# Where the split weights of eleven projections stand in SBUF, seen from the split activations

## The chip, the cores and the metric

One core of one Trainium2 chip runs the whole program. The metric is device time in microseconds (us) of that core; less is better.

## The reference

Two transformer-like blocks on one sequence of 512 tokens with 1024 features, all in float32. The first block has a sparse-attention mixer with gates, a feed-forward network, a gated linear recurrence and a second feed-forward network; the second has differential attention, a mixture of experts, an RWKV mixer and a second mixture of experts. Between them stand large dense projections of the form `h @ w`, and eleven of them are what this case is about:

```
proj = h @ w_in                     # nsa_in:  1024 -> 2560 (+48 gates)
o @ w_out                           # nsa_out: 1024 -> 1024
silu(h @ w_gate) * (h @ w_up)       # ffn_in, twice:  1024 -> 2 x 2816
(...) @ ffn_w_out                   # ffn_out, twice: 2816 -> 1024
h @ w_in                            # rg_in:   1024 -> 2 x 1408
(...) @ w_out                       # rg_out:  1408 -> 1024
x @ w_qkv                           # da_in:   1024 -> 3072
o @ w_o                             # da_out:  1024 -> 1024
(y * g) @ w_o                       # rw_out:  1024 -> 1024
```

## The kernel before

Everything is kept transposed: features on the 128 partitions, in chunks of 128, and the 512 tokens along the free dimension. A projection is computed by the helper `dense` (line 128). To get float32 accuracy out of float32r matmuls it splits both operands into a high part (a float32r copy) and a low part (what is left): weights into `whi` and `wlo`, activations into `xhi` and `xlo`. Per chunk of 128 input features and 128 output features it issues three matmuls of 128x128 weights against 128x512 activations into one PSUM bank: high by high (line 212), high weights by low activations (line 213), low weights by high activations (line 214):

```
nc.tensor.matmul(ps[0:width, slot * tiles + o], high, xhi[:, k], start=(k == 0), stop=False)
nc.tensor.matmul(ps[0:width, slot * tiles + o], high, xlo[:, k], start=False, stop=False)
last = nc.tensor.matmul(ps[0:width, slot * tiles + o], low, xhi[:, k], start=False, stop=(k == kt - 1))
```

Each matmul is preceded by the load of its own weights, which TensorE does while the matmul before it streams its activations. The weights are the stationary operand (128 columns of 4 bytes, 512 bytes of a partition), the activations the moving one (512 columns, 2048 bytes).

The weights come tile by tile, n tiles a projection, in two slots. SyncE issues the DMA of a tile once the slot's last split is done; ScalarE copies it into `whi[:, slot]`; VectorE subtracts that into `wlo[:, slot]`; TensorE waits for the split (`lo_done`), multiplies, and signals `products_done`; ScalarE or VectorE takes the result from PSUM. A projection can have a head: the first chunks of its first tile, split earlier into tiles of their own (`early.hi` and `early.lo`, named nsa_in_h0, da_in_h0 and so on), so that it can begin without a wait. `stay_busy` (line 329) issues bf16 matmuls of 512 columns before a projection.

Tiles are placed in SBUF in the order in which the code asks for them, each behind the one before (a few from the right end). Where a tile stands, in bytes of a partition modulo 512, is called its line here. The distance is that of `whi` or `wlo` from `xhi` and `xlo`, modulo 512. All four are whole multiples of 512 bytes long, chunk by chunk as well, so one distance holds for all chunks of a projection. Before the change it is 0 in all eleven. In the feed-forward network an unused tile sees to that: between `xlo` and `whi` stand 32 bytes of a coefficient tile, 4096 of `silu` and 480 of `ffn{layer}_to_line` (line 613), together 4608, nine times 512. A similar one, `rg_to_line` (line 1240), stands in the recurrence. The heads stand at 0 as well, but for that of da_in, which lies at the right end: da_in_h0 at byte 219104 and da_in_xhi at 174624, which is 448 modulo 512.

Three other groups of float32r matmuls with 512 columns play a part in the prediction, all in the compression stage after nsa_in. The gate projection (lines 774 to 776) has 48 columns a chunk, so its weights step by 192 bytes while the activations step by 2048; the first chunk stands at 0. The headed spreads (lines 757 and 758) multiply a 24x128 one-hot tile, `cp_heads`, with the split reciprocals `cp_rhi` and `cp_rlo`; the distance is 128 throughout.

Of the kernel before, what the change touches and what calls it, by code (L numbers as in the profile page):

```python
# [14 lines left out]
F32 = mybir.dt.float32  # L15
# [4 lines left out]
P = 128  # L20
SEQ = 512
D = 1024
KD = D // P
# [6 lines left out]
KR = RNN // P  # L30
# [94 lines left out]
                sp.dma_start(dst, src).then_inc(self.second_loaded, 16)  # L125


def dense(B, name, n, tiles, kt, kp, width, loads, x, act_body=None, dve_body=None, unrolled=False, xhi=None, xlo=None, is_split=False, pool_body=None, dve_head=None, norm=None, early=None, sp_tail=None, slots=None, coming=None, busy=(0, 0, 0)):

# [10 lines left out]
    nc, ACT, ALU = B.nc, B.ACT, B.ALU  # L142
    with ExitStack() as st:
        if slots is None:
            w2 = st.enter_context(nc.sbuf_tensor(name + "_w", [kp, 2, kt, tiles * width], F32))
            slots = (w2[:, 0], w2[:, 1])
        whi = st.enter_context(nc.sbuf_tensor(name + "_whi", [kp, 2, kt, tiles * width], F32R))
        wlo = st.enter_context(nc.sbuf_tensor(name + "_wlo", [kp, 2, kt, tiles * width], F32R))
        if xhi is None:
            xhi = st.enter_context(nc.sbuf_tensor(name + "_xhi", [kp, kt, SEQ], F32R))  # L150
        if xlo is None:
            xlo = st.enter_context(nc.sbuf_tensor(name + "_xlo", [kp, kt, SEQ], F32R))
# [425 lines left out]
def add_mixed(B, layer, part, tiles=2):  # L578

    nc, ALU = B.nc, B.ALU  # L580

    def body(dve, i, slot, ps):
        for o in range(tiles):
            x = B.xT[:, bass.ds(i * tiles + o, 1)]
            nc.vector.scalar_tensor_tensor(out=x, in0=ps[:, o:o + 1], scalar=B.gate_col(layer, part, i * tiles + o), in1=x,
                                           op0=ALU.mult, op1=ALU.add)
    return body


def ffn(B, layer, next_weights=None):  # L590
    nc, A, ACT, ALU = B.nc, B.A, B.ACT, B.ALU
    w_in = A["ffn_w_in"][layer].rearrange("(k p) n -> p k n", p=P)
    w_out = A["ffn_w_out"][layer].rearrange("(k p) n -> p k n", p=P)
    KF = FFN // P
    with ExitStack() as st:

        with ExitStack() as s2:
            normed = s2.enter_context(nc.sbuf_tensor(f"ffn{layer}_normed", [P, KD, SEQ], F32))
            rstd = s2.enter_context(nc.sbuf_tensor(f"ffn{layer}_rstd", [P, SEQ], F32))
        hhi = st.enter_context(nc.sbuf_tensor(f"ffn{layer}_hhi", [P, KF, SEQ], F32R))  # L600
        hlo = st.enter_context(nc.sbuf_tensor(f"ffn{layer}_hlo", [P, KF, SEQ], F32R))

        came = st.enter_context(nc.sbuf_tensor(f"ffn{layer}_came", [P, 2 * KD * 2 * P], F32))
        in_slots = tuple(came[:, q * KD * 2 * P:(q + 1) * KD * 2 * P].rearrange("p (k n) -> p k n", k=KD) for q in range(2))
        out_first = came[:, 0:KF * P].rearrange("p (k n) -> p k n", k=KF)
        out_loads = lambda w, i: [(w[:, :, :], w_out[:, :, bass.ds(i * P, P)])]
        early = EarlyWeights(B, f"ffn{layer}_out", st, KF, P, out_loads, out_first, head=KD)
        with ExitStack() as s2:
            xhi = s2.enter_context(nc.sbuf_tensor(f"ffn{layer}_xhi", [P, KD, SEQ], F32R))
            xlo = s2.enter_context(nc.sbuf_tensor(f"ffn{layer}_xlo", [P, KD, SEQ], F32R))  # L610
            norm = RmsModulate(B, f"n2_{layer}", s2, "norm2_g", layer, 3, normed, rstd[:])
            gated = s2.enter_context(nc.sbuf_tensor(f"ffn{layer}_silu", [P, 2, SEQ], F32))
            s2.enter_context(nc.sbuf_tensor(f"ffn{layer}_to_line", [P, 120], F32))
            h = gated
            h_chain = B.sem(f"ffn{layer}_h_chain")

            def loads(w, i):
                return [(w[:, :, 0:P], w_in[:, :, bass.ds(i * P, P)]),
                        (w[:, :, P:2 * P], w_in[:, :, bass.ds(i * P + FFN, P)])]

            def product(dve, i, slot, ps):
                nc.vector.tensor_tensor(h[:, slot], gated[:, slot], ps[:, 1], ALU.mult).then_inc(h_chain, 1)  # L622
                dve.wait_ge(h_chain, i * 2 + 1)
                row = lambda T: T[:, bass.ds(i, 1)].rearrange("p o t -> p (o t)")
                nc.vector.tensor_copy(row(hhi), h[:, slot]).then_inc(h_chain, 1)
                dve.wait_ge(h_chain, i * 2 + 2)
                nc.vector.tensor_tensor(row(hlo), h[:, slot], row(hhi).bitcast(F32), ALU.subtract)
            dense(B, f"ffn{layer}_in", KF, 2, KD, P, P, loads, None, busy=(6, 3, 8),
                  act_body=lambda i, slot, ps: nc.scalar.activation(gated[:, slot], ps[:, 0], ACT.Silu),  # L629
                  dve_body=product, xhi=xhi, xlo=xlo, norm=norm, sp_tail=early.load, slots=in_slots, coming=early)  # L630
        out_second = st.enter_context(nc.sbuf_tensor(f"ffn{layer}_out_w1", [P, KF, P], F32))
        coming = next_weights() if next_weights else None
        dense(B, f"ffn{layer}_out", KD, 1, KF, P, P,
              out_loads, None, dve_body=add_mixed(B, layer, 5, tiles=1), xhi=hhi, xlo=hlo, is_split=True, early=early, slots=(out_first, out_second[:]),
              sp_tail=coming.load if coming else None, coming=coming)


def nsa(B):
# [6 lines left out]
    nc, A, ACT, ALU = B.nc, B.A, B.ACT, B.ALU  # L645
    w_in = A["nsa_w_in"][0].rearrange("(k p) n -> p k n", p=P)
# [10 lines left out]
    with ExitStack() as st:  # L657
# [7 lines left out]
        norm = RmsModulate(B, "n1_0", x_scope, "norm1_g", 0, 0, projT[:, 12:20], projT[:, 11], summed_early=True)  # L665
# [16 lines left out]
        def clear(pool):  # L682
# [3 lines left out]
            for T in (kcz, vcz):  # L686
                nc.gpsimd.memset(T[:], 0.0)

        dense(B, "nsa_in", 10, 2, KD, P, P, loads, None, busy=(0, 0, 8), unrolled=True, xhi=xhi, xlo=xlo, norm=norm, early=early, pool_body=clear, sp_tail=small_loads,
              act_body=lambda i, slot, ps: nc.scalar.activation(projT[:, 2 * i:2 * i + 2], ps, ACT.Copy))  # L690


# [235 lines left out]
        out_first = st.enter_context(nc.sbuf_tensor("nsa_out_w2", [P, KD, 256], F32))  # L928
        early = EarlyWeights(B, "nsa_out", st, KD, 256, out_loads, head=KD // 2, second=True)
        nsa_attention(B, projT, kz, kcz, vnat, vcz, gates, ohi, olo, early)  # L930
        dense(B, "nsa_out", 4, 2, KD, P, P, out_loads, None, dve_body=add_mixed(B, 0, 2), xhi=ohi, xlo=olo, is_split=True, early=early, slots=(out_first[:], early.second[:]))


def nsa_attention(B, projT, kz, kcz, vnat, vcz, gates, ohi, olo, early):
# [279 lines left out]
def rg_lru(B):  # L1214
# [7 lines left out]
    with ExitStack() as st:  # L1222
# [11 lines left out]
        xhi = yhi[:, 0:KD]  # L1234
# [75 lines left out]

        def pad(dve):
            nc.vector.memset(raw[:, :, 0:PAD], 0.0).then_inc(conv_chain, 1)
        dense(B, "rg_in", KR, 2, KD, P, P, busy=(3, 3, 12), loads=lambda w, i: [(w[:, :, 0:P], w_in[:, :, i * P:(i + 1) * P]),
                            (w[:, :, P:2 * P], w_in[:, :, i * P + RNN:(i + 1) * P + RNN])],
              x=None, act_body=take, dve_body=convolve, xhi=xhi, xlo=xlo, unrolled=True, norm=RmsModulate(B, "n1_1", x_scope, "norm1_g", 1, 0, gT[:, 0:KD], conv[:, KR - 1]), pool_body=load_band, dve_head=pad, slots=(came[:].rearrange("p (k n) -> p k n", k=KD), in_second[:]))
        x_scope.close()
# [1 line left out]
        with ExitStack() as s2:  # L1318
# [144 lines left out]
            def _(dve):  # L1463
# [56 lines left out]
                                            B.cols("ada_b", (8 + h) * KD, KD).rearrange("p (t j) -> p t j", j=2), ALU.add)  # L1520
        scope.close()
        dense(B, "rg_out", KD, 1, KR, P, P,
              out_loads, None, busy=(0, 0, 3), dve_body=add_mixed(B, 1, 2, tiles=1), xhi=yhi, xlo=ylo, is_split=True, early=early)


ALPHA = (2 * 2) ** 0.25
# [2 lines left out]
def add_deepnorm(B):  # L1529

    nc, ALU = B.nc, B.ALU

    def body(dve, i, slot, ps):
        x = B.xT[:, bass.ds(i * 2, 2)]
        return nc.vector.scalar_tensor_tensor(out=x, in0=x, scalar=ALPHA, in1=ps, op0=ALU.mult, op1=ALU.add)
    return body


def qkv_loads(B):
    w_qkv = B.A["attn_w_qkv_2"][0].rearrange("(k p) n -> p k n", p=P)  # L1540
    return lambda w, i: [(w[:, :, :], w_qkv[:, :, bass.ds(i * 256, 256)])]
# [36 lines left out]
def diff_attention(B, early_in, right):  # L1578
# [8 lines left out]
    with ExitStack() as st:  # L1587
# [4 lines left out]
        with ExitStack() as s2:  # L1592
            sb = lambda name, shape: s2.enter_context(nc.sbuf_tensor("da_" + name, shape, F32))
            projT = sb("projT", [P, 24, SEQ])
            odd = right.enter_context(nc.sbuf_tensor("da_in_w1", [P, KD, 256], F32, side="right"))
            dense(B, "da_in", 12, 2, KD, P, P, qkv_loads(B), B.xT, early=early_in, slots=(early_in.w[:], odd[:]),
                  act_body=lambda i, slot, ps: nc.scalar.activation(projT[:, bass.ds(i * 2, 2)], ps, ACT.Copy, scale=SC if i < 4 else 1.0),
                  unrolled=True)
            right.close()
# [173 lines left out]
            def _(dve):  # L1773
# [84 lines left out]
        units = right.enter_context(nc.sbuf_tensor("da_moe_units", [P, AHEAD, HID // P, D], F32, side="right"))  # L1858
        B.ahead = [units[:, u] for u in range(AHEAD)]
        dense(B, "da_out", KD // 2, 2, KD, P, P,  # L1860
              out_loads, None, busy=(0, 0, 3), dve_body=add_deepnorm(B), xhi=ohi, xlo=olo, is_split=True, early=early, sp_tail=lambda sp: ask_gate_and_up(B, sp, 0, B.ahead))


def norm_moe(B, layer, gain, bias, mixer=None):
# [1099 lines left out]
def rwkv(B, dest, gate, AR):  # L2964
# [11 lines left out]
    with ExitStack() as st:  # L2976
# [22 lines left out]
        def out_loads(wt, i):  # L2999
# [3 lines left out]
        early = EarlyWeights(B, "rw_out", st, KD, 256, out_loads, tile=quarters(Bt)[:, 0], head=KD // 2)  # L3003
        B.ahead = [AR[:, u].rearrange("p (k a) n -> p k (a n)", a=2) for u in range(AHEAD)]
        rwkv_result(B, AR, K, Vn, bonus, mixed_g, g_w1, ohi, olo, early)
        dense(B, "rw_out", KD // 2, 2, KD, P, P, out_loads, None, busy=(0, 0, 3), dve_body=add_deepnorm(B), xhi=ohi, xlo=olo, is_split=True, early=early,
              slots=(quarters(K)[:, 0], quarters(K)[:, 1]), sp_tail=lambda sp: ask_gate_and_up(B, sp, 1, B.ahead))


# [616 lines left out]
```

## Time and profile before

| what | value |
|---|---|
| median of 3 runs | 3282.23 us (3279.44 to 3285.97) |
| span of the profiled execution | 3277.8 us |
| time of the profiled execution around its span | not given; the median is 4.4 us over the span |
| TensorE busy | 2920.2 us, 89% |
| VectorE, ScalarE, GpSimd busy | 1310.6, 887.2, 264.2 us |
| mean granted TensorE clock | 0.956 |

The span is that of one execution, from the first to the last instruction. Matmul durations overlap, since a matmul enters the array while the one before it is still draining; the time from one start to the next is the rate at which they are done. Starts in the order of time are given to 0.01 us, so rates are read over several matmuls. The granted clock is a share of 2.4 GHz.

### The profile page before, as it was taken

The numbers are of one execution on the slowest core, as the hardware profiler recorded it, in microseconds if no ns is written. First come the engines' busy times: TensorE is split into PE (matmuls) and PEld (weight loads), VectorE is DVE, ScalarE is ACT, GpSimd is POOL, SyncE is SP. The second block draws the span as 40 slices with busy tenths as digits, with TensorE's granted clock in tenths as the row PEclk, the third lists the DMA queues.
The fourth block names the chain that finished last, engine by engine and source line by source line (L and its number), as shares of the span: only waits on it lengthen the run. The fifth ranks groups of instructions, "written<-read, shape, count | busy, mean of one in ns | idle before, by whom it ended". The sixth has DMA issues, their size and how long they took to land. (4 is left out here: it accounts for less than half of the span.)

```text
span 3277.8 us, 66493 instructions
## 1 busy us (share of the span) xinstructions
PE 2920.2 (89%) x27826; PEld 2116.8 (65%) x27826; DVE 1310.6 (40%) x2356; ACT 887.2 (27%) x1564; POOL 264.2 (8%) x344
## 2 busy tenths in 40 slices
PE   7999999999998999999988997775888998997876
PEld 5766678878764788787756664443467866664453
DVE  3265543331656433322374221112596564221213
ACT  3245522221445222212362000003342333000002
POOL 1014300000400000000000000001121430000001
PEclk9999999999998999999999999887899999999998
DMA  8335233331426333423307999998122217999997
GB/s 211 79 113 200 75 80 95 97 101 53 121 64 228 85 100 94 109 66 103 110 25 285 375 396 427 425 428 312 39 58 81 47 33 288 391 426 425 426 426 293
DMA packets 378062, 638.64 MB, mean 195 GB/s; under 512 B 90693, under 2 KB 327922, under 8 KB 343802
## 3 DMA queue, kind: packets, MB, share of 16 engines
q1 hardware_dynamic: 352329, 601.98, 50.4%
q10 hardware_dynamic: 21264, 23.88, 2.1%
q0 software_dynamic: 4256, 9.68, 0.8%
q8 instruction: 166, 2.72, 0.3%
q14 instruction: 47, 0.38, 0.0%
HBM read 611.06 MB, written 24.38 MB: 194 GB/s over the span
## 5 line engine op out<-in xcount | busy, mean ns | idle before, releaser
L2296 DVE TENSOR_TENSOR moe_scratch<-moe_scratch,moe_ps 128x128 f32<-128x128 f32 x102 | 39.4, 386 | 652.6 <-ACT moe_scratch L2153 652.6
L212 PE MATMUL ffn_in_ps<-ffn_xhi,ffn_in_whi 128*128 128x512 f32 x704 | 274.4, 390 | 6.3 <-DVE ffn_xlo L417 4.5
L2095 PE MATMUL moe_ps<-moe_ring,moe_scratch 128*32 128x256 f32 x3360 | 213.4, 404 | 69.0 <-DMA moe_ring<-in_moe_w_gu 58.3
L213 PE MATMUL ffn_in_ps<-ffn_xlo,ffn_in_whi 128*128 128x512 f32 x704 | 274.1, 389 | 0.0
L214 PE MATMUL ffn_in_ps<-ffn_xhi,ffn_in_wlo 128*128 128x512 f32 x704 | 274.0, 389 | 0.0
L2095 PEld LDWEIGHTS moe_ps<-moe_ring,moe_scratch 128*32 128x32 f32 x3360 | 126.0, 115 | 150.6 <-issue 63.0
L2080 PE MATMUL moe_ps<-xT,moe_hot 128*32 128x256 f32 x3296 | 202.6, 384 | 0.0
L2153 ACT ACTIVATE moe_scratch<-moe_ps 128x128 f32<-128x128 f32 x102 | 28.3, 277 | 503.7 <-PE moe_ps L2095 501.7
L2080 PEld LDWEIGHTS moe_ps<-xT,moe_hot 128*32 128x32 f32 x3296 | 122.4, 113 | 62.2 <-issue 8.7
L212 PEld LDWEIGHTS ffn_in_ps<-ffn_xhi,ffn_in_whi 128*128 128x128 f32 x704 | 132.2, 188 | 35.3 <-issue 5.4
L213 PEld LDWEIGHTS ffn_in_ps<-ffn_xlo,ffn_in_whi 128*128 128x128 f32 x704 | 132.2, 188 | 27.4
L214 PEld LDWEIGHTS ffn_in_ps<-ffn_xhi,ffn_in_wlo 128*128 128x128 f32 x704 | 132.2, 188 | 27.3
L622 DVE TENSOR_TENSOR ffn_silu<-ffn_silu,ffn_in_ps 128x512 f32<-128x512 f32 x44 | 30.3, 688 | 282.1 <-ACT ffn_silu L629 282.1
L2095 PE MATMUL moe_ps<-da_moe_units,moe_scratch 128*32 128x256 f32 x1600 | 107.6, 421 | 37.0 <-DMA da_moe_units<-in_moe_w_gu 33.7
L2157 ACT ACTIVATE moe_y<-moe_ps 128x256 f32<-128x256 f32 x102 | 39.1, 383 | 356.1 <-PE moe_ps L2105 356.1
L2105 PE MATMUL moe_ps<-moe_ring,moe_scratch 128*32 128x256 f32 x1952 | 119.4, 383 | 16.4 <-issue 16.0
L213 PE MATMUL ffn_out_ps<-ffn_hlo,ffn_out_whi 128*128 128x512 f32 x336 | 130.8, 389 | 0.0
L212 PE MATMUL ffn_out_ps<-ffn_hhi,ffn_out_whi 128*128 128x512 f32 x336 | 130.8, 389 | 0.0
L214 PE MATMUL ffn_out_ps<-ffn_hhi,ffn_out_wlo 128*128 128x512 f32 x336 | 130.8, 389 | 0.0
L629 ACT ACTIVATE ffn_silu<-ffn_in_ps 128x512 f32<-128x512 f32 x44 | 26.3, 597 | 359.2 <-PE ffn_in_ps L214 359.2
L2095 PE MATMUL moe_ps<-rw_AR,moe_scratch 128*32 128x256 f32 x1504 | 94.5, 400 | 28.5 <-DMA rw_AR<-in_moe_w_gu 25.2
L2095 PEld LDWEIGHTS moe_ps<-da_moe_units,moe_scratch 128*32 128x32 f32 x1600 | 62.7, 119 | 76.5 <-issue 35.0
(788 smaller groups left out, 6006.1 us busy)
## 6 DMA issues: line engine op xcount, KB each, us to landing
moe_ring<-in_moe_w_gu SPq DMA_DIRECT2D x74, 2048.0 KB, 36.6
moe_ring<-in_moe_w_down SPq DMA_DIRECT2D x38, 2048.0 KB, 34.8
da_moe_units<-in_moe_w_gu SPq DMA_DIRECT2D x27, 2048.0 KB, 31.2
rw_AR<-in_moe_w_gu SPq DMA_DIRECT2D x27, 2048.0 KB, 29.0
ffn_came<-in_ffn_w_in SPq DMA_DIRECT2D x88, 512.0 KB, 5.0
da_moe_units<-in_moe_w_down SPq DMA_DIRECT2D x13, 2048.0 KB, 37.4
rw_AR<-in_moe_w_down SPq DMA_DIRECT2D x13, 2048.0 KB, 33.4
na_modw<-in_ada_w SPq DMA_DIRECT2D x6, 4096.0 KB, 13.6
```

The lines of the kernel that those rows point to most:

```text
L212: nc.tensor.matmul(ps[0:width, slot * tiles + o], high, xhi[:, k], start=(k == 0), stop=False)
L213: nc.tensor.matmul(ps[0:width, slot * tiles + o], high, xlo[:, k], start=False, stop=False)
L214: last = nc.tensor.matmul(ps[0:width, slot * tiles + o], low, xhi[:, k], start=False, stop=(k == kt - 1))
L622: nc.vector.tensor_tensor(h[:, slot], gated[:, slot], ps[:, 1], ALU.mult).then_inc(h_chain, 1)
L629: act_body=lambda i, slot, ps: nc.scalar.activation(gated[:, slot], ps[:, 0], ACT.Silu),
L2080: last = nc.tensor.matmul(psX[j * BLK:(j + 1) * BLK].rearrange("p (q n) -> p q n", q=2), hot[:, c], rows_of(c)[:, j::4], start=(c == 0), s ...
L2095: last = nc.tensor.matmul(psGU[j * BLK:(j + 1) * BLK].rearrange("p (g a n) -> p g a n", g=2, a=2), xbT[:, k], cols[:, j], start=(k == 0), ...
L2105: last = nc.tensor.matmul(psY[j * BLK:(j + 1) * BLK], hT[:, k * BLK:(k + 1) * BLK], unit(PARTS * e + 2)[:, k, j * 256:(j + 1) * 256], star ...
L2153: nc.scalar.activation(gated, psG, ACT.Silu).then_inc(silu_done, 1)
L2157: nc.scalar.activation(y[:, s], psY, ACT.Copy).then_inc(y_taken, 1)
L2296: V.tensor_tensor(h.rearrange("p (a m i) -> p a i m", a=2, m=2), gated.rearrange("p (a i m) -> p a i m", a=2, m=2), psU.rearrange("p (a i ...
```

## The change

`dense` gets a parameter `apart`, two numbers of bytes. The first is left unused ahead of `whi`, the second ahead of `wlo`; where `dense` places `xhi` itself, as in da_in alone of the eleven, it leaves as much again ahead of `xhi` as brings that back to its line. The tile `ffn{layer}_to_line` goes. The calls pass these values:

```diff
+        def leave(what, line):
+            if line:
+                st.enter_context(nc.sbuf_tensor(f"{name}_before_{what}", [kp, line // 4], F32))
+        leave("whi", apart[0])
         whi = st.enter_context(nc.sbuf_tensor(name + "_whi", [kp, 2, kt, tiles * width], F32R))
+        leave("wlo", apart[1])
         wlo = st.enter_context(nc.sbuf_tensor(name + "_wlo", [kp, 2, kt, tiles * width], F32R))
         if xhi is None:
+            leave("xhi", (1024 - apart[0] - apart[1]) % 512 if apart[0] + apart[1] else 0)
             xhi = st.enter_context(nc.sbuf_tensor(name + "_xhi", [kp, kt, SEQ], F32R))
...
-            s2.enter_context(nc.sbuf_tensor(f"ffn{layer}_to_line", [P, 120], F32))
...
 ffn_in:   apart=(32, 0) if layer == 0 else (416, 0)
 ffn_out:  apart=(256, 0) if layer == 0 else (96, 0)
 nsa_in:   apart=(128, 0)
 nsa_out:  apart=(384, 0)
 rg_in:    apart=(192, 0)
 rg_out:   apart=(320, 0)
 da_in:    apart=(0, 256)
 da_out:   apart=(256, 256)
 rw_out:   apart=(160, 0)
```

(The last nine lines list the new argument of each call; nothing else in the calls changes.) The heads' own tiles keep their places, and so do the raw weight tiles, the activations handed to `dense`, and everything outside it. The RWKV input projections have code of their own and are not touched.

## Rows read from the trace of the kernel before

**Rows 1.** The page, parts 1 and 2: TensorE's busy time, by 40 slices

```profile
PE 2920.2 (89%) x27826; PEld 2116.8 (65%) x27826; DVE 1310.6 (40%) x2356; ACT 887.2 (27%) x1564; POOL 264.2 (8%) x344
...
PE   7999999999998999999988997775888998997876
```

**Rows 2.** Windows over the projections, three rows and the header; the sum is of eleven

```profile
core 0: us, PE busy (x) PEld busy (x) DVE busy (x) ACT busy (x) POOL busy (x), PEclk, DMA share, GB/s
...
455.40:690.00 234.60, 233.68 (x1030) 193.30 (x1031) 93.91 (x98) 57.16 (x50) 0.00 (x0) 1.00 0.34 95
...
1495.30:1619.20 123.90, 123.90 (x548) 102.38 (x546) 22.94 (x10) 29.35 (x21) 0.00 (x0) 1.00 0.23 75
...
sum 1253.50, PE 1248.75 PEld 1030.84 DVE 429.03 ACT 286.31 POOL 23.08; mean PE 113.52 PEld 93.71 DVE 39.00 ACT 26.03 POOL 2.10
```

**Rows 3.** Line 214: who waited for it (us, times)

```profile
  ACT ffn_silu L629: 359.2, 44
```

**Rows 4.** Line 212 on TensorE: counts, durations in ns (min/median/max), first and last start

```profile
L212 PE MATMUL ffn_in_ps<-ffn_xhi,ffn_in_whi x704: 387/389/497, 455.4 to 1356.8; 128*128 128x512 f32 x176
L212 PE MATMUL ffn_out_ps<-ffn_hhi,ffn_out_whi x336: 388/389/390, 706.2 to 1481.2; 128*128 128x512 f32 x168
L212 PE MATMUL da_in_ps<-da_in_xhi,da_in_whi x188: 388/389/767, 1488.2 to 1618.5; 128*128 128x512 f32 x188
L212 PE MATMUL rg_in_ps<-rg_yhi,rg_in_whi x176: 388/389/766, 833.4 to 953.8; 128*128 128x512 f32 x176
L212 PE MATMUL nsa_in_ps<-nsa_xhi,nsa_in_whi x146: 388/389/398, 56.1 to 154.7; 128*128 128x512 f32 x146
L212 PE MATMUL rg_out_ps<-rg_yhi,rg_out_whi x88: 388/389/497, 1042.8 to 1102.1; 128*128 128x512 f32 x88
L212 PE MATMUL nsa_out_ps<-nsa_ohi,nsa_out_whi x56: 388/389/394, 399.5 to 439.6; 128*128 128x512 f32 x56
L212 PE MATMUL da_out_ps<-da_ohi,da_out_whi x56: 388/389/395, 1718.8 to 1758.9; 128*128 128x512 f32 x56
L212 PE MATMUL rw_out_ps<-rw_ohi,rw_out_whi x56: 388/389/390, 2711.9 to 2752.0; 128*128 128x512 f32 x56
```

**Rows 5.** In order of time, da_in's first tile; 1493.77 to 1495.14 loads the head

```profile
1493.77 0.39 PE L214 MATMUL da_in_ps<-da_in_xhi,da_in_wlo 128*128 128x512 f32 x1
...
1495.14 0.39 PE L214 MATMUL da_in_ps<-da_in_xhi,da_in_l 128*128 128x512 f32 x1
...
1501.94 0.39 PE L214 MATMUL da_in_ps<-da_in_xhi,da_in_wlo 128*128 128x512 f32 x1
```

**Rows 6.** Groups of instructions, 1493.9 to 1495.3 us (busy us, mean ns)

```profile
L213 PE MATMUL da_in_ps<-da_in_xlo,da_in_h 128*128 128x512 f32 x2 | 0.8, 394 | 0.0
L212 PE MATMUL da_in_ps<-da_in_xhi,da_in_h 128*128 128x512 f32 x2 | 0.8, 392 | 0.0
```

**Rows 7.** In order of time, the gate projection, second and last of its 24 matmuls

```profile
162.83 0.39 PE L775 MATMUL cp_psT<-nsa_xlo,cp_whi_g 128*48 128x512 f32 x1
...
167.88 0.39 PE L776 MATMUL cp_psT<-nsa_xhi,cp_wlo_g 128*48 128x512 f32 x1
```

**Rows 8.** In order of time, rg_out after a stall: matmuls 2, 8 and 15

```profile
1043.13 0.39 PE L213 MATMUL rg_out_ps<-rg_ylo,rg_out_whi 128*128 128x512 f32 x1
...
1044.52 0.39 PE L213 MATMUL rg_out_ps<-rg_ylo,rg_out_whi 128*128 128x512 f32 x1
...
1046.11 0.39 PE L214 MATMUL rg_out_ps<-rg_yhi,rg_out_wlo 128*128 128x512 f32 x1
```

**Rows 9.** In order of time, headed spreads, second and last of a run of 8

```profile
189.72 0.38 PE L758 MATMUL cp_psD<-cp_rlo,cp_heads 24*128 24x512 f32 x1
...
191.12 0.39 PE L758 MATMUL cp_psD<-cp_rlo,cp_heads 24*128 24x512 f32 x1
```

**Rows 10.** In order of time, six of the helper's bf16 matmuls

```profile
451.32 1.46 PE L332 MATMUL ffn_in_ps<-ident_b 128*128 128x512 bf16 x6
```

**Rows 11.** Groups of instructions, 451.1 to 452.75 us (busy us, mean ns)

```profile
L332 PE MATMUL ffn_in_ps<-ident_b 128*128 128x512 bf16 x7 | 1.7, 379 | 0.0
```

More of the change, by code:

```diff
@@ L125, in load, with dense @@
                 sp.dma_start(dst, src).then_inc(self.second_loaded, 16)
-def dense(B, name, n, tiles, kt, kp, width, loads, x, act_body=None, dve_body=None, unrolled=False, xhi=None, xlo=None, is_split=False, pool_body=None, dve_head=None, norm=None, early=None, sp_tail=None, slots=None, coming=None, busy=(0, 0, 0)):
+def dense(B, name, n, tiles, kt, kp, width, loads, x, act_body=None, dve_body=None, unrolled=False, xhi=None, xlo=None, is_split=False, pool_body=None, dve_head=None, norm=None, early=None, sp_tail=None, slots=None, coming=None, busy=(0, 0, 0), apart=(0, 0)):
     nc, ACT, ALU = B.nc, B.ACT, B.ALU
@@ L627, in product @@
                 nc.vector.tensor_tensor(row(hlo), h[:, slot], row(hhi).bitcast(F32), ALU.subtract)
-            dense(B, f"ffn{layer}_in", KF, 2, KD, P, P, loads, None, busy=(6, 3, 8),
+            dense(B, f"ffn{layer}_in", KF, 2, KD, P, P, loads, None, busy=(6, 3, 8), apart=(32, 0) if layer == 0 else (416, 0),
                   act_body=lambda i, slot, ps: nc.scalar.activation(gated[:, slot], ps[:, 0], ACT.Silu),
@@ L633, in ffn @@
         dense(B, f"ffn{layer}_out", KD, 1, KF, P, P,
-              out_loads, None, dve_body=add_mixed(B, layer, 5, tiles=1), xhi=hhi, xlo=hlo, is_split=True, early=early, slots=(out_first, out_second[:]),
+              out_loads, None, apart=(256, 0) if layer == 0 else (96, 0), dve_body=add_mixed(B, layer, 5, tiles=1), xhi=hhi, xlo=hlo, is_split=True, early=early, slots=(out_first, out_second[:]),
               sp_tail=coming.load if coming else None, coming=coming)
@@ L687, in clear @@
                 nc.gpsimd.memset(T[:], 0.0)
-        dense(B, "nsa_in", 10, 2, KD, P, P, loads, None, busy=(0, 0, 8), unrolled=True, xhi=xhi, xlo=xlo, norm=norm, early=early, pool_body=clear, sp_tail=small_loads,
+        dense(B, "nsa_in", 10, 2, KD, P, P, loads, None, apart=(128, 0), busy=(0, 0, 8), unrolled=True, xhi=xhi, xlo=xlo, norm=norm, early=early, pool_body=clear, sp_tail=small_loads,
               act_body=lambda i, slot, ps: nc.scalar.activation(projT[:, 2 * i:2 * i + 2], ps, ACT.Copy))
@@ L930, in nsa @@
         nsa_attention(B, projT, kz, kcz, vnat, vcz, gates, ohi, olo, early)
-        dense(B, "nsa_out", 4, 2, KD, P, P, out_loads, None, dve_body=add_mixed(B, 0, 2), xhi=ohi, xlo=olo, is_split=True, early=early, slots=(out_first[:], early.second[:]))
+        dense(B, "nsa_out", 4, 2, KD, P, P, out_loads, None, apart=(384, 0), dve_body=add_mixed(B, 0, 2), xhi=ohi, xlo=olo, is_split=True, early=early, slots=(out_first[:], early.second[:]))
 def nsa_attention(B, projT, kz, kcz, vnat, vcz, gates, ohi, olo, early):
@@ L1312, in pad @@
             nc.vector.memset(raw[:, :, 0:PAD], 0.0).then_inc(conv_chain, 1)
-        dense(B, "rg_in", KR, 2, KD, P, P, busy=(3, 3, 12), loads=lambda w, i: [(w[:, :, 0:P], w_in[:, :, i * P:(i + 1) * P]),
+        dense(B, "rg_in", KR, 2, KD, P, P, apart=(192, 0), busy=(3, 3, 12), loads=lambda w, i: [(w[:, :, 0:P], w_in[:, :, i * P:(i + 1) * P]),
                             (w[:, :, P:2 * P], w_in[:, :, i * P + RNN:(i + 1) * P + RNN])],
@@ L1522, in rg_lru @@
         dense(B, "rg_out", KD, 1, KR, P, P,
-              out_loads, None, busy=(0, 0, 3), dve_body=add_mixed(B, 1, 2, tiles=1), xhi=yhi, xlo=ylo, is_split=True, early=early)
+              out_loads, None, apart=(320, 0), busy=(0, 0, 3), dve_body=add_mixed(B, 1, 2, tiles=1), xhi=yhi, xlo=ylo, is_split=True, early=early)
 ALPHA = (2 * 2) ** 0.25
@@ L1595, in diff_attention @@
             odd = right.enter_context(nc.sbuf_tensor("da_in_w1", [P, KD, 256], F32, side="right"))
-            dense(B, "da_in", 12, 2, KD, P, P, qkv_loads(B), B.xT, early=early_in, slots=(early_in.w[:], odd[:]),
+            dense(B, "da_in", 12, 2, KD, P, P, qkv_loads(B), B.xT, apart=(0, 256), early=early_in, slots=(early_in.w[:], odd[:]),
                   act_body=lambda i, slot, ps: nc.scalar.activation(projT[:, bass.ds(i * 2, 2)], ps, ACT.Copy, scale=SC if i < 4 else 1.0),
@@ L1860, in diff_attention @@
         dense(B, "da_out", KD // 2, 2, KD, P, P,
-              out_loads, None, busy=(0, 0, 3), dve_body=add_deepnorm(B), xhi=ohi, xlo=olo, is_split=True, early=early, sp_tail=lambda sp: ask_gate_and_up(B, sp, 0, B.ahead))
+              out_loads, None, apart=(256, 256), busy=(0, 0, 3), dve_body=add_deepnorm(B), xhi=ohi, xlo=olo, is_split=True, early=early, sp_tail=lambda sp: ask_gate_and_up(B, sp, 0, B.ahead))
 def norm_moe(B, layer, gain, bias, mixer=None):
@@ L3005, in rwkv @@
         rwkv_result(B, AR, K, Vn, bonus, mixed_g, g_w1, ohi, olo, early)
-        dense(B, "rw_out", KD // 2, 2, KD, P, P, out_loads, None, busy=(0, 0, 3), dve_body=add_deepnorm(B), xhi=ohi, xlo=olo, is_split=True, early=early,
+        dense(B, "rw_out", KD // 2, 2, KD, P, P, out_loads, None, apart=(160, 0), busy=(0, 0, 3), dve_body=add_deepnorm(B), xhi=ohi, xlo=olo, is_split=True, early=early,
               slots=(quarters(K)[:, 0], quarters(K)[:, 1]), sp_tail=lambda sp: ask_gate_and_up(B, sp, 1, B.ahead))
```

## The prediction, made blind

> **What bounds the kernel now.** I began with the page's busy shares: TensorE is busy for 89% of the span, and in most of the 40 slices for 9 tenths [rows 1]. The chain that ended last covers only the closing microseconds and gives nothing for a change spread over the middle. So I went to the stretches of the eleven projections by windows [rows 2]. In the first feed-forward stretch TensorE is busy 233.68 of 234.60 us, in the attention projection 123.90 of 123.90, in all eleven together 1248.75 of 1253.50, with the granted clock at 1.00, its 2.4 GHz level, in both. VectorE and ScalarE are busy a third and a quarter of that time, DMA 0.23 to 0.34. The waits agree: of what waits for the last matmul of a product, ScalarE's SiLU alone waits 359.2 us in 44 goes [rows 3]. In these stretches every nanosecond added to each matmul-to-matmul step moves the end. Only what comes before a projection's first products, the split of its first tile, lies outside that.
>
> A step is the time from one matmul's start to the next's. A 128x512 matmul has a duration of 389 ns in every projection [rows 4], but they overlap. The step is read from starts: 30 steps between 1495.14 and 1501.94 us take 6.80 us, 226.7 ns each [rows 5]. There the weights being loaded stand at distance 0 (modulo 512) from the activations being streamed, as everywhere in the projections but in one head. The second projection I tried gives the same: seven steps in 1.59 us, 227 ns, once it has settled [rows 8].
>
> **The change, part by part.** It adds no instruction, wait, transfer or engine hop; it adds and takes away unused bytes between tiles. DMA targets keep their places (the raw weight tiles are placed ahead of the pads), so SyncE's and GpSimd's queues see the same work. VectorE and ScalarE split the weights at other addresses; should that cost them something, it is hidden under TensorE, since they are busy 429 and 286 us of 1253.5 [rows 2]. Without that cover only each projection's first tile counts, at most a few tenths of a us in eleven places; I take 0. What is left is the step of every matmul whose weights are loaded from another distance than that of the activations streaming meanwhile.
>
> How many: one line issues one matmul per weight chunk, and three lines share it. By line 212's counts [rows 4], times three: the ffn inputs 2112 (half at 64, half at 448), the ffn outputs 1008 (256 and 96), nsa_in 438 (128), nsa_out 168 (384), rg_in 528 (192), rg_out 264 (320), rw_out 168 (160); together 4686. In da_in only the low weights move, by 256: 188. In da_out the high ones stand at 256 and the low ones at 512, which is 0 again: 2 x 56 = 112. Sum 4986 loads. The 58 head chunks, which lie in tiles of their own, keep their distance (14 in nsa_in, 8 in each of three outputs, 8 in each ffn output, 4 in da_in).
>
> What one costs: the trace has three places where float32r weights are loaded at another distance.
> - The nearest: da_in's first tile keeps two head chunks at 448, in the middle of a running stream, with 128x128 weights and the same activations. Six steps, 1493.77 to 1495.14 us, take 1.37 us, 228.3 each, and the stream is back at 226.7 at once [rows 5]. That is +1.7 ns, with +-1.7 from rounding; durations in those steps also leave 389, at 392 and 394 [rows 6]. Exactly this distance is what the second ffn input gets.
> - The gate projection: 48 columns a chunk, so its chunks run through 0, 192, 384, 64, 256, 448, 128, 320. Its 22 steps from 162.83 to 167.88 us take 5.05 us, 229.5 each, +2.9 [rows 7]. That goes through all the multiples of 64 that the change uses, with the unsettled start in it.
> - The headed spreads (24 rows, distance 128): six steps in 1.40 us, 233 ns, +6.6 [rows 9]. But a stream at distance 0 is no better just after a stall: its first six full steps take 1.39 us, 231.7 each, before it settles [rows 8]. These short runs never get that far, so this is a high bound.
>
> The lower bound is none or a gain: the helper's bf16 512-column matmuls have five steps in 1.46 - 0.38 = 1.08 us, 216 each [rows 10, 11], 10.7 ns less than float32r. If the 10.7 were collisions between weight reads and streaming reads at distance 0, another distance could give them back; nothing here excludes that, but no stretch at another distance shows a mean under 228. I take +2.3 ns, the middle of the two running streams (1.7 and 2.9). 4986 x 2.3 ns = **11.5 us**.
>
> There is a rule that speaks against any cost. The Trainium skill, TensorE: Matmul & The Clock Gate, in "Step-by-step: what each phase is for", says that TensorE has two independent SBUF read ports, so loading the next weights doesn't take read bandwidth from the running matmul. By that rule the step wouldn't know of the distance, the sum would be 0 and the time 3282; the head chunks of da_in lean against it, though by little more than the rounding.
>
> Beyond TensorE: a projection that ends later shifts all behind it. The expert stages after da_out and rw_out are fed by DMA issued at the end of these projections' splits, and could swallow their part: 112 + 168 loads, 0.6 us. I leave it in. The sum is made against the profiled execution, whose span is 3277.8; the median of the runs is 3282.23, 4.4 more for what lies around the span and for spread. Added to the median: 3282.2 + 11.5 = **3293.7 us**.
>
> **The rivals.** What a measurement can tell from no change here is about 0.2%, 6.6 us, which is 1.3 ns a load.
> 1. *The stream never settles.* At distance 0 the first steps after a stall take 231.7 and then fall to 226.7 [rows 8]; if that settling is a phase that only distance 0 lets the loads find, all other projections stay at the unsettled rate, +5.0 to +6.6 ns: 25 to 33 us, 3307 to 3315. For it: the headed spreads [rows 9], and in the gate rows steps still don't equalise after twelve. Against it: 228.3 at 448.
> 2. *No effect.* What shows in rows 5 and 7 would come from a distance that changes from one load to the next; at any constant distance the stream would settle as at 0. Then 3282, and this is also what comes out if the pads miss their aim. They don't by my arithmetic: the ffn input loses 480 bytes and gains 32 or 416, so 64 and 448 from before's 0.
> 3. *Faster.* Distance 0 is itself the collision, and others run freely at up to bf16's 216: up to -10.7 x 4986 = -53 us, 3229. It decides once the mean load gains 1.3 ns. For it: the gap between the two types, 227 against 216. Against it: the gap has a plainer reason (four bytes an element against two), and no other distance was under 228 in the mean.
>
> **How the numbers follow.** Forecast (+0.8 to +4.5 ns, 3286 to 3305) 0.50; rival 1, 0.22; rival 2, 0.20; rival 3, 0.06; 0.02 for the rest. Slower by over 0.2%: nearly all of the forecast's case and rival 1, 0.73. Within 0.2%: rival 2 and the forecast's low end, 0.21. Faster 0.06. The range runs from the no-effect case, 3281, to the middle of rival 1, 3312.
>
> **What would show it.** In the after-profile: the same instruction counts on all engines; 30 steps of da_in from 6.80 us to about 6.85 (only the low weights move), an ffn_in stretch of 30 steps at 6.87; windows over the two ffn inputs longer by some 2 to 3 us each, their end being where the difference adds up; stages between projections the same to the microsecond. Steps of 231 throughout say rival 1, 226.7 in all eleven say rival 2, less than 226 anywhere says rival 3. If the sizes differ much between projections, the distance itself sets the price, and my one price for all was the mistake. Time lost between projections instead of in them would overturn the whole account.

## The result: 22.5 us slower, nearly all of it in the matmul steps

The changed kernel takes 3303.36 us (median of 4 runs, 3297.99 to 3313.36) against 3280.84 for the one before on the same chip: a ratio of 1.0068, 95% interval 1.0053 to 1.0083, so 17 to 27 us slower. The forecast was slower, 3293.7, with a range of 3281 to 3312.

The page of the profile after, its span and busy times:

```profile
span 3303.9 us, 66493 instructions
PE 2949.9 (89%) x27826; PEld 2119.7 (64%) x27826; DVE 1310.1 (40%) x2356; ACT 887.7 (27%) x1564; POOL 263.5 (8%) x344
```

Against [rows 1] all counts are the same, and VectorE, ScalarE and GpSimd are busy for the same time within 1 us. Only TensorE is busy longer, by 29.7 us; of these 21.3 lie in the eleven projections (the sums below), the rest between them, where the granted clock differs a little from execution to execution (0.92 after against 0.96 before between da_in and da_out).

Windows over the eleven projections after, each from its first matmul's start to its last one's end, in the order nsa_in, nsa_out, first ffn_in, first ffn_out, rg_in, rg_out, second ffn_in, second ffn_out, da_in, da_out, rw_out (columns as in [rows 2]):

```profile
45.20:157.90 112.70, 111.82 (x481) 90.23 (x480) 29.18 (x22) 29.81 (x24) 0.00 (x0) 1.00 0.47 83
400.40:445.10 44.70, 44.70 (x192) 36.04 (x192) 12.33 (x10) 6.70 (x4) 0.00 (x0) 1.00 0.25 48
460.30:708.50 248.20, 248.16 (x1056) 198.51 (x1056) 93.99 (x98) 57.14 (x51) 0.00 (x0) 0.99 0.33 90
711.30:832.60 121.30, 121.27 (x528) 99.99 (x528) 28.93 (x15) 19.60 (x8) 0.00 (x0) 0.99 0.31 83
845.20:967.40 122.20, 121.35 (x528) 98.94 (x528) 74.38 (x92) 44.05 (x56) 22.94 (x44) 1.00 0.31 83
1054.80:1116.60 61.80, 61.80 (x264) 49.51 (x264) 17.40 (x15) 9.67 (x7) 0.00 (x0) 1.00 0.28 80
1130.40:1374.00 243.60, 243.54 (x1056) 199.36 (x1056) 94.00 (x98) 57.18 (x50) 0.00 (x0) 0.99 0.33 91
1376.80:1502.00 125.20, 125.16 (x528) 100.37 (x528) 29.53 (x16) 20.24 (x9) 0.00 (x0) 0.99 0.33 89
1504.50:1639.20 134.70, 132.72 (x576) 109.09 (x576) 31.00 (x19) 35.34 (x29) 0.00 (x0) 0.99 0.27 86
1736.50:1782.80 46.30, 46.30 (x194) 37.71 (x192) 11.77 (x7) 5.95 (x4) 0.00 (x0) 0.95 0.57 213
2731.90:2778.40 46.50, 46.45 (x194) 36.99 (x192) 11.77 (x8) 6.09 (x4) 0.00 (x0) 0.97 0.58 220
sum 1307.20, PE 1303.28 PEld 1056.74 DVE 434.29 ACT 291.78 POOL 22.94; mean PE 118.48 PEld 96.07 DVE 39.48 ACT 26.53 POOL 2.09
```

The same windows in the kernel before, both ffn_in, the second ffn_out, and the sum of the eleven (the windows of [rows 2] are cut a little shorter):

```profile
455.40:696.30 240.90, 239.94 (x1056) 198.16 (x1056) 93.91 (x98) 57.17 (x51) 0.00 (x0) 1.00 0.33 92
...
1116.80:1357.60 240.80, 239.88 (x1056) 198.13 (x1056) 93.87 (x98) 57.19 (x50) 0.00 (x0) 1.00 0.34 92
1360.50:1482.10 121.60, 121.56 (x528) 100.16 (x528) 29.53 (x17) 20.22 (x9) 0.00 (x0) 0.99 0.33 92
...
sum 1284.90, PE 1282.01 PEld 1056.41 DVE 434.12 ACT 291.55 POOL 22.68; mean PE 116.55 PEld 96.04 DVE 39.47 ACT 26.50 POOL 2.06
```

The projections are 22.3 us longer, of 26.1 us by which the spans differ; the other 3.8 lie between them: five stretches are longer, by 0.3 to 1.8 and 4.9 in all, and the rest give 1.1 back. That is within what one kernel's executions differ by (3279.0 to 3286.0 us before). And the cost is very uneven. The first ffn_in (distance 64) pays 7.3 us; the second, the same work at 448, pays 2.8; the second ffn_out (96) 3.6; the first ffn_out (256) and da_in nothing.

In order of time, one matmul and the thirtieth after it, in the first ffn_in, the second ffn_in and the second ffn_out of the changed kernel:

```profile
559.90 0.39 PE L218 MATMUL ffn_in_ps<-ffn_xhi,ffn_in_whi 128*128 128x512 f32 x1
...
566.90 0.39 PE L218 MATMUL ffn_in_ps<-ffn_xhi,ffn_in_whi 128*128 128x512 f32 x1
```

```profile
1199.84 0.39 PE L220 MATMUL ffn_in_ps<-ffn_xhi,ffn_in_wlo 128*128 128x512 f32 x1
...
1206.71 0.39 PE L220 MATMUL ffn_in_ps<-ffn_xhi,ffn_in_wlo 128*128 128x512 f32 x1
```

```profile
1439.96 0.40 PE L218 MATMUL ffn_out_ps<-ffn_hhi,ffn_out_whi 128*128 128x512 f32 x1
...
1446.99 0.39 PE L218 MATMUL ffn_out_ps<-ffn_hhi,ffn_out_whi 128*128 128x512 f32 x1
```

Thirty steps take 7.00, 6.87 and 7.03 us, where [rows 5] has 6.80: 233.3, 229.0 and 234.3 ns a step against 226.7. The mean of all steps of a projection, from the starts in the trace without the head and the first eighth of the rest, gives the price of each distance (extra is over 226.67):

| projection | distance | step, ns | extra x steps | us |
|---|---|---|---|---|
| first ffn_in | 64 | 233.33 | 6.67 x 1056 | 7.0 |
| second ffn_out | 96 | 234.29 | 7.62 x 504 | 3.8 |
| nsa_in | 128 | 232.36 | 5.69 x 438 | 2.5 |
| second ffn_in | 448 | 228.89 | 2.22 x 1056 | 2.3 |
| rg_out | 320 | 233.32 | 6.65 x 264 | 1.8 |
| rg_in | 192 | 228.89 | 2.22 x 528 | 1.2 |
| rw_out | 160 | 233.33 | 6.67 x 168 | 1.1 |
| nsa_out | 384 | 232.38 | 5.71 x 168 | 1.0 |
| first ffn_out | 256 | 226.67 | 0 | 0 |
| da_in | high 0, low 256 | 226.67 | 0 | 0 |
| da_out | high 256, low 0 | 226.67 | 0 | 0 |

Sum 20.7 us, of the 22.3 by which the windows grew; most of the rest is da_out, 1.4 us longer at an unchanged step. It begins with ten steps of about 427 ns at a granted clock of 0.50, the 1.2 GHz level, where before there were three; seven more at 200 ns extra each are those 1.4 us. The table already hints at a rule: distances that differ by 256 (64 and 320, 128 and 384, 192 and 448, 0 and 256) cost the same.

### The profile page after: what moved, and what is told of

Same layout as the page of the kernel before. It is cut to its first block and busy times, and to the rows that moved or that the text cites. A ratio compares the mean times of both kernels' runs of the same rounds, so it can differ in the third digit from the quotient of the medians.

```text
span 3303.9 us, 66493 instructions
## 1 busy us (share of the span) xinstructions
PE 2949.9 (89%) x27826; PEld 2119.7 (64%) x27826; DVE 1310.1 (40%) x2356; ACT 887.7 (27%) x1564; POOL 263.5 (8%) x344
## 5 line engine op out<-in xcount | busy, mean ns | idle before, releaser
L220 PEld LDWEIGHTS ffn_in_ps<-ffn_xhi,ffn_in_wlo 128*128 128x128 f32 x704 | 132.8, 189 | 29.7
```

## The experiments

The theory going in: the step of a stream depends on the distance between split weights and split activations modulo 256, the same for every projection, and that is all of the 22 us. The rivals: the projection sets the price and not the distance; the period is 512; the time went elsewhere and the steps only accompany it. A further question was which pair has to be in line: a load with what streams beside it, or a matmul's own weights with its own activations.

**All at 256.** Every projection with the weights half a line away:

```diff
-... apart=(128, 0) ...      # nsa_in, and likewise in the other calls
+... apart=(256, 0) ...      # ffn_in: (224, 0), since 32 bytes are there already
```

> Split weights of all eleven projections at distance 256. Theory (the step depends on the distance between the weights being loaded and the activations streaming meanwhile, taken modulo 256): every projection steps at 226.7 ns and the time is that of before, 3281 within 3 us. Rival (256 was free in two projections by their kind, since ffn_out of the first layer and da_out take the results on VectorE, and not by the distance): ffn_in, nsa_in and rg_in step at 229 or more, and the time is 10 us or more over before.

Measured: 3285.21 us (12 runs) against 3282.76, ratio 1.0005, interval 0.9991 to 1.0019. The medians are 2.4 us apart, which is inside the interval (-3 to +6 us). All eleven step at 226.67. Thirty steps of the first ffn_in:

```profile
559.90 0.39 PE L218 MATMUL ffn_in_ps<-ffn_xhi,ffn_in_whi 128*128 128x512 f32 x1
...
566.70 0.39 PE L218 MATMUL ffn_in_ps<-ffn_xhi,ffn_in_whi 128*128 128x512 f32 x1
```

6.80 us, as at distance 0. The rival that 256 was free only in those two kinds of projection falls. It also clears the bytes themselves: the weights of every projection stand elsewhere than before, and it costs nothing that can be told.

**All at 96.**

```diff
-... apart=(128, 0) ...      # nsa_in, and likewise in the other calls
+... apart=(96, 0) ...       # ffn_in: (64, 0)
```

> All eleven at 96, the dearest distance so far (234.3 ns a step in the second ffn_out). Theory: all 5418 loads outside the heads pay 7.6 ns, 41 us; 3322 us, and every projection steps at 234.3. Rival (a price of the projection, not of the distance): steps differ between projections as in the changed kernel, so nsa_in 232.4, ffn_in 233.3 and 228.9, rg_in 228.9, and the sum stays near 25 us, 3306.

Measured: 3321.88 us, ratio 1.0134, interval 1.0103 to 1.0165, which is 44 us (34 to 54) against 41 expected; the two medians are 39 apart. Every projection steps at 234.28 or 234.29. The counts, durations and first and last starts of two of them:

```profile
L218 PE MATMUL nsa_in_ps<-nsa_xhi,nsa_in_whi x146: 390/397/401, 55.9 to 157.8; 128*128 128x512 f32 x146
L218 PE MATMUL rg_out_ps<-rg_yhi,rg_out_whi x88: 392/397/496, 1060.2 to 1121.4; 128*128 128x512 f32 x88
```

nsa_in has 145 x 3 steps in 101.9 us, 234.3 each; in [rows 4] they took 98.6, 226.7 each. One distance, one price: a price of the projection is refuted, and time follows the steps to within the interval. Nor does it matter on which line the activations stand, as long as all the weights are equally far from them: modulo 512 they begin at 0 in rw_out, 288 in nsa_out, 320 in nsa_in and 32 in the others.

**The first ffn_in back at 0**, the rest as changed:

```diff
-... apart=(32, 0) if layer == 0 else (416, 0),
+... apart=(480, 0) if layer == 0 else (416, 0),
```

> The changed kernel with only the first layer's ffn_in back at distance 0 (from 64). Theory: 1056 loads give back 6.7 ns each, 7.0 us; 3296 against 3303. Rival (the time went elsewhere, with the placing of tiles or between projections): less than 3 us come back although the steps there do.

Measured: 3297.75 us (12 runs), ratio 1.0047, interval 1.0029 to 1.0064, where the changed kernel has 1.0068: 0.0021, 6.9 us, came back, for 7.0 expected. The two intervals overlap, so the time alone is only consistent with it; the trace shows the first ffn_in at 226.67 again and the stretch at 240.9 us instead of 248.2, all others as in the table. Thirty of its steps take 6.80 us:

```profile
559.63 0.39 PE L218 MATMUL ffn_in_ps<-ffn_xhi,ffn_in_whi 128*128 128x512 f32 x1
...
566.43 0.39 PE L218 MATMUL ffn_in_ps<-ffn_xhi,ffn_in_whi 128*128 128x512 f32 x1
```

**The other multiples of 32**, one in each projection (nsa_in 32, nsa_out 480, first ffn_in 224, second 288, first ffn_out 352, second 416, rg_in 64, rg_out 448, da_in 96, da_out 128, rw_out 192). The edit is the numbers in `apart` again.

> Other distances in each projection: nsa_in 32, nsa_out 480, first ffn_in 224, second 288, first ffn_out 352, second 416, rg_in 64, rg_out 448, da_in 96, da_out 128, rw_out 192. Theory (distance modulo 256, the same for every projection): rg_in steps at 233.3, rg_out at 228.9, da_in and the first ffn_out (352) at 234.3, the second ffn_out (416, that is 160) at 233.3, da_out 232.4, rw_out 228.9; nsa_in and the second ffn_in (32 and 288) agree with each other, nsa_out and the first ffn_in (480 and 224) too. Rival (modulo 512): 352, 416 and 288 have prices of their own. Rival (the projection sets it): rg_in stays at 228.9, rw_out and rg_out at 233.

Measured, from one execution (3317.19 us): 32 and 288 step at 233.33; 224 and 480 at 233.3; 352 at 234.29 like 96; 416 at 233.33 like 160; rg_in at 64 233.33, rg_out at 448 228.89, da_in at 96 234.28, da_out at 128 232.38, rw_out at 192 228.89. Two of the rows behind it, rg_out at 448 and nsa_in at 32:

```profile
L218 PE MATMUL nsa_in_ps<-nsa_xhi,nsa_in_whi x146: 392/395/499, 55.7 to 157.3; 128*128 128x512 f32 x146
L218 PE MATMUL rg_out_ps<-rg_yhi,rg_out_whi x88: 394/394/505, 1065.4 to 1125.3; 128*128 128x512 f32 x88
```

rg_out's 87 x 3 steps take 59.9 us here, 229.5 each with the start, and took 61.2 at 96; nsa_in's 145 x 3 take 101.6, 233.6 each with the start. Each projection took the price of its new distance. The theory holds for all multiples of 32, with a period of 256 and not 512:

| distance modulo 256 | 0 | 32 | 64 | 96 | 128 | 160 | 192 | 224 |
|---|---|---|---|---|---|---|---|---|
| step, ns | 226.67 | 233.33 | 233.33 | 234.29 | 232.4 | 233.33 | 228.89 | 233.33 |

**Finer distances.** `whi` and `wlo` become slices of tiles 512 bytes larger, so that they can begin at any 4 bytes:

```diff
+        def set_off(what):
+            size = 2 * kt * tiles * width
+            skip = apart[0] // 4
+            raw = st.enter_context(nc.sbuf_tensor(f"{name}_{what}", [kp, 128 + size], F32R))
+            return raw[:, skip:skip + size].rearrange("p (s k n) -> p s k n", s=2, k=kt)
+        whi = set_off("whi")
+        wlo = set_off("wlo")
```

> Distances closer than 32 to 0 modulo 256: nsa_in 16, nsa_out 8, first ffn_in 240, second 248, first ffn_out 4, second 252, rg_in 272, rg_out 264, da_in 24, da_out 232, rw_out 12. Theory: 226.7 is the floor of this load and stream, nothing is under it; distances within a few elements of 0 are free or nearly, and pairs 16 and 272, 8 and 264 agree. Rival 3 of the prediction (0 collides and a small offset would not): some distance steps under 226, down to the 216 of the bf16 matmuls, and that would make the kernel faster than before by up to 50 us.

Measured (3296.01 us, one execution):

| distance modulo 256 | 4 | 8 | 12 | 16 | 24 | 232 | 240 | 248 | 252 |
|---|---|---|---|---|---|---|---|---|---|
| step, ns | 232.38 | 230.65 | 226.66 | 233.33 | 230.00 | 231.11 | 226.67 | 233.33 | 226.67 |

Thirty steps at distance 4, and thirty at 252, the first and the second ffn_out:

```profile
760.06 0.39 PE L217 MATMUL ffn_out_ps<-ffn_hhi,ffn_out_whi 128*128 128x512 f32 x1
...
767.03 0.39 PE L217 MATMUL ffn_out_ps<-ffn_hhi,ffn_out_whi 128*128 128x512 f32 x1
```

```profile
1440.03 0.39 PE L217 MATMUL ffn_out_ps<-ffn_hhi,ffn_out_whi 128*128 128x512 f32 x1
...
1446.83 0.39 PE L217 MATMUL ffn_out_ps<-ffn_hhi,ffn_out_whi 128*128 128x512 f32 x1
```

They take 6.97 and 6.80 us. Half of the expectation held: 226.67 is the floor, met at 12, 240 and 252 and never passed, and 8 agrees with 264 (230.65 and 230.66), 16 with 272 (233.33 both). The other half fell: a few bytes off are not nearly free. One element (4 bytes) on one side costs 5.7 ns and on the other nothing. The price is no smooth function of the distance.

**High and low parts at different distances.** Several settings at once, in different projections (numbers in `apart`, and unused bytes ahead of `xlo` in the first ffn_in and in da_in); rg_out, da_out and rw_out are back at 0:

```diff
+            if layer == 0:
+                s2.enter_context(nc.sbuf_tensor(f"ffn{layer}_before_xlo", [P, 16], F32))
             xlo = s2.enter_context(nc.sbuf_tensor(f"ffn{layer}_xlo", [P, KD, SEQ], F32R))
...
+            leave("xlo", 64 if name == "da_in" else 0)
             xlo = st.enter_context(nc.sbuf_tensor(name + "_xlo", [kp, kt, SEQ], F32R))
```

> High and low parts at different distances; 64 unless said, all else 0. Theory (what counts is the activations that stream while the weights are loaded: high weights are loaded under xhi both times, low weights under xlo): first ffn_in with the low weights and xlo both moved by 64 steps at 226.7, as if nothing had moved; second ffn_in and nsa_out with the low weights alone moved, and da_in with xlo alone moved, have one load in three off and step at 227 to 230; nsa_in and rg_in with the high weights alone moved have two in three off and step at 229 to 233. Rival 1 (a matmul's own weights against its own activations): the first ffn_in has two of three off (high by xlo, low by xhi) and steps at 229 to 233, more than the second. Rival 2 (distance between successive weights): the first and second ffn_in step alike, over 227.

Measured (3307.91 us, one execution): the first ffn_in, `wlo` and `xlo` both moved, 232.2, where the theory said 226.7; the second and nsa_out, `wlo` alone, 231.1 both; da_in, `xlo` alone, 232.0; nsa_in 233.33 and rg_in 231.11, with the same distances, `whi` alone moved. Two settings were not in the expectation: the first ffn_out with `wlo` alone at 96 steps at 232.6, the second with `whi` alone at 96 at 230.0, so that there two loads in three off line cost less than one in three. The three at 0 step at 226.67. Of the ranges expected, those for one load in three off (227 to 230) were all passed, and nsa_in lies just over its 229 to 233. Each load of the first ffn_in had the activations beside it in line, and it paid all the same:

```profile
559.98 0.40 PE L220 MATMUL ffn_in_ps<-ffn_xlo,ffn_in_whi 128*128 128x512 f32 x1
...
566.95 0.40 PE L220 MATMUL ffn_in_ps<-ffn_xlo,ffn_in_whi 128*128 128x512 f32 x1
```

Thirty steps, 6.97 us. So the first form of my theory, the load against the stream beside it, fell. Rival 2, the distance between successive weights, wants the two ffn_in alike, and they are 1.1 ns apart; da_in pays with all its weights in line. Rival 1, a matmul's own pair, ranks the two ffn_in rightly, but no rule that knows these distances alone can tell nsa_in from rg_in.

**Two products, to keep the pairs apart.**

```diff
+                    if name in ("ffn0_in", "ffn1_in", "da_in"):
+                        crossed = name == "ffn1_in"
+                        nc.tensor.matmul(ps[0:width, slot * tiles + o], high, (xlo if crossed else xhi)[:, k], start=(k == 0), stop=False)
+                        last = nc.tensor.matmul(ps[0:width, slot * tiles + o], low, (xhi if crossed else xlo)[:, k], start=False, stop=(k == kt - 1))
+                        continue
```

> Both ffn_in with the low weights and xlo moved by 64, and only two products a chunk, so that pairs can be kept apart; all other projections at 0. The first ffn_in computes high by xhi and low by xlo (the two mixed products are left out): each matmul's own pair stands at 0, while every load streams beside activations 64 away. The second computes high by xlo and low by xhi (high by high is left out): own pairs stand 64 away, every load stands at 0 from what streams beside it. da_in computes high by xhi and low by xlo with everything at 0, as the control for two products: 226.7. Theory 1 (what counts is the load against the stream beside it): first ffn_in 229 to 234, second 226.7. Theory 2 (a matmul's own weights against its own activations): first 226.7, second 229 to 234. Theory 3 (both count, a load's place in the stream being set by the ones before it): both over 228.

Measured: both ffn_in step at 231.67, da_in at 226.66. Thirty steps in the first, then in the second:

```profile
560.05 0.40 PE L220 MATMUL ffn_in_ps<-ffn_xhi,ffn_in_whi 128*128 128x512 f32 x1
...
566.99 0.40 PE L220 MATMUL ffn_in_ps<-ffn_xhi,ffn_in_whi 128*128 128x512 f32 x1
```

```profile
1199.96 0.39 PE L220 MATMUL ffn_in_ps<-ffn_xlo,ffn_in_whi 128*128 128x512 f32 x1
...
1206.91 0.40 PE L220 MATMUL ffn_in_ps<-ffn_xlo,ffn_in_whi 128*128 128x512 f32 x1
```

6.94 and 6.95 us. With only the own pairs in line, or only the loads in line with the stream beside them, the price is the same 5.0 ns. Theories 1 and 2 each wanted one of the two at 226.7 and fall; of theory 3 it is shown that neither kind of pair alone is enough. That the two prices are equal is not explained: in both, successive weights stand 64 apart, and so do successive activations, and these were not varied apart from the rest. (The whole kernel's 3097 us is short because work is left out, and says nothing here.)

**The mixed distances once more**, the kernel of that experiment unchanged, on another chip.

> The kernel with mixed distances once more. There nsa_in and rg_in have the same distances (high weights 64 away, low ones at 0) and settled at 233.3 and 231.1. Theory (where distances differ from load to load there are several steady patterns, and the way in which the stream starts picks one): at least one projection settles at another mean than in the first execution. Rival (something in the projection or its place fixes it): all eleven means are the same again, nsa_in 233.3 and rg_in 231.1 included.

Measured: all eleven means are the same again to 0.01 ns, nsa_in 233.33 and rg_in 231.11 included, and the whole took 3301.82 us. The theory, which wanted another mean somewhere, fell. But the pattern behind a mean is not fixed: by the starts in the trace nsa_in's settled steps ran 229, 235, 236 ns in the first execution and 229, 233, 233, 234, 236, 235 in this one, 233.33 in the mean both times. The durations (minimum, median, maximum) show it too, the first execution above, this one below:

```profile
L219 PE MATMUL nsa_in_ps<-nsa_xhi,nsa_in_whi x146: 398/398/501, 55.0 to 157.4; 128*128 128x512 f32 x146
...
L219 PE MATMUL nsa_in_ps<-nsa_xhi,nsa_in_whi x146: 394/396/401, 56.0 to 157.5; 128*128 128x512 f32 x146
```

What separates nsa_in from rg_in is fixed in the kernel and was not found; the activations of nsa_in begin at 320 and those of rg_in at 32, modulo 512, which was not varied by itself.

## Why the prediction was right or wrong

- **The bound**: right. TensorE's steps in the eleven projections set the end; 22.3 of 26.1 us of the span lie there, and no other engine changed. The splits on ScalarE and VectorE cost nothing at their new addresses: both engines are busy as long as before in the eleven windows (291.8 and 434.3 us against 291.6 and 434.1). The DMA share is not 0.23 to 0.34 in all eleven, as the prediction has it, but up to 0.59 in da_out and rw_out; nothing hangs on it.
- **The count of loads**: the arithmetic is right, but 804 of the 4986 counted as dear stood at 256, which is free: 504 in the first ffn_out, 188 in da_in, 112 in da_out. So da_in's thirty steps stayed at 6.80 us. (The 6.85 forecast for them is a slip besides: ten loads at 2.3 ns make 6.82.)
- **The term that was mis-sized** is "I take +2.3 ns, the middle of the two running streams". The mean over the 4986 loads was 20.7 us / 4986 = 4.2 ns, so 20.7 us instead of 11.5; over the 4182 that paid at all it was 5.0. The reading for 448 was good: +1.7 with a rounding of 1.7, and 2.22 measured. Wrong was to carry the price of one distance to all; the prediction's own signs name that as its mistake. 448 and 192 are the cheapest of the multiples of 32 that cost anything, while 64, 96, 160 and 320, over 1992 of the steps, cost 6.7 to 7.6.
- **Luck**: that the time lies in the range owes something to the choice of distances, free and cheap ones beside dear ones. The same price of 2.3 ns on all 5418 loads at 96 would have given 12.5 us, where the medians showed 39, beyond the range; at 256 it would have given the same 12.5, where nothing that can be told was measured.
- **A row was there and was explained away.** The headed spreads at 128 [rows 9] showed 233 ns; I took that for the unsettled start of a short run. The settled price of 128 is 232.4. The unsettled steps at distance 0 [rows 8] happen to be as long, 231.7, and I let the one explain the other. The gate projection [rows 7] mixes all distances chunk by chunk, with 48 columns, and told nothing of a stream at one distance.
- **Rival 1**, no settling, was nearer in the money (25 to 33 us, where the time grew by 22.5) and close for the dearer distances (5.0 to 6.6 ns, where 6.7 to 7.6 were measured), but not as told: these streams do settle, each into a repeating pattern, only at a longer mean. At 64 every step is 233 or 234; at 160 the three lines take 231, 231 and 238.
- **Rival 2**, no effect, is refuted by the time as by the steps. The rule behind it, from the Trainium skill, TensorE: Matmul & The Clock Gate, "Step-by-step: what each phase is for", that loading the next weights takes nothing from the running matmul, does not cover this: in a stream of alternating loads and float32r matmuls, placing alone changes the step by up to 7.6 ns in 226.7. The measurement decides.
- **Rival 3**, faster, is refuted for these shapes: none of 17 distances modulo 256, nor the mixed ones, gave a mean under 226.66. None of these distances gives back any of the 10.7 ns to the bf16 matmuls' 216; what makes up that gap was not tried.

Open stays why the step depends on the distance. Shown is that it does, with a period of 256 bytes at every multiple of 32 and at 8 and 16; that a settled stream keeps its mean; and that, at 64 bytes off, having only a matmul's own pairs in line, or only each load and the stream beside it, is not enough. No mechanism in the reads of SBUF was shown.

## What to carry to other kernels

Where TensorE runs float32r matmuls back to back with a weight load for each (shown here for 128x128 weights, 512 columns and the 2.4 GHz level of the clock), place the stationary and the moving tiles at the same address modulo 256, the high and low parts of both included; a few hundred unused bytes do it, and in this kernel leaving it undone cost 0.7% as changed and 1.3% with all at 96. Look for it by the distance of starts over thirty matmuls, since durations (medians of 389 ns against 393 to 398) and busy shares (89% both times) hardly show it, and don't read one distance's price as another's: 4 bytes can cost as much as 128.

## What the runs showed of the hardware that I had not expected

- With all weights equally far from all activations, the step is a function of that distance modulo 256 bytes, and a jagged one: 226.67 at 0, 12, 240 and 252, 232.4 at 4, 233.3 at 16, 228.9 at 192, 234.3 at 96.
- Settled streams repeat a short pattern (three steps at 160 and 192, seven at 96), and such a stream has the same mean in each projection with the same distance, whichever of the lines 0, 32, 288 and 320 its activations are on. At 96 eleven projections agreed to 0.01 ns, though the split of the seven steps differs between them (231, 234, 235, 234, 231, 238, 237 in one; 230, 235, 235, 233, 232, 237, 238 in another).
- With mixed distances two projections with the same distances settled at 233.33 and 231.11, and did so again in a second execution, nsa_in there by another pattern of steps.
- Two ways of being half in line cost the same: 231.67 with only the own pairs in line, and 231.67 with only load and neighbouring stream in line.
